# Seven block products for the third factor of a short convolution's input projection

## What is computed

```python
def short_conv_mixer(h, w_in, conv_w, w_out):
    bcx = h @ w_in                       # 512x1024 @ 1024x3072
    b_gate, c_gate, xp = bcx[..., :D], bcx[..., D:2*D], bcx[..., 2*D:]
    u = c_gate * xp
    u_conv = causal_depthwise_conv(u, conv_w)      # 3 taps along the tokens
    return (b_gate * u_conv) @ w_out

def swiglu(h, w_gate, w_up, w_down):
    return (silu(h @ w_gate) * (h @ w_up)) @ w_down

# layer 0: h = h + attention(rms_norm(h)); h = h + swiglu(rms_norm(h))
# layer 1: h = h + short_conv_mixer(rms_norm(h)); h = h + swiglu(rms_norm(h));  out = rms_norm(h)
```

## Time and profile before

| what | value |
|---|---|
| median of 3 runs | 1074.52 us (1074.01 to 1074.58) |
| the profiled execution, its own time | 1073.69 us |
| span of its instructions | 1071.9 us |
| PE busy | 1061.5 us, 99% of the span |
| PEld, DVE, ACT, POOL busy | 949.9, 777.4, 486.3, 40.5 us |
| chain of work that ended last | PE 91% |
| mean granted clock of TensorE | 0.996 of full speed |

### The profile page before, as it was taken

One profiled execution on the slowest core, in us unless ns is written; L12 is line 12 of the kernel. 1 busy time (PEld: TensorE's weight loads), 2 busy tenths in 40 slices (PEclk: granted clock), 3 DMA queues, 4 the chain that ended last, 5 costly groups with the idle time before them and its releaser, 6 DMA issues.

```text
span 1071.9 us, 17102 instructions
## 1 busy us (share of the span) xinstructions
PE 1061.5 (99%) x6496; PEld 949.9 (89%) x6496; DVE 777.4 (73%) x1081; ACT 486.3 (45%) x684; POOL 40.5 (4%) x22
## 2 busy tenths in 40 slices
PE   9999999999999999999999999999999999999997
PEld 7888888889999999888888888888999999988886
DVE  5667775999999998643457456779999999873343
ACT  6586663745554555422131212355545544651221
POOL 0232220000000000000000000000000000000000
PEclk9999999999999999999999999999999999999998
DMA  8221112232233322323322332322332233223301
GB/s 287 98 69 49 50 69 72 86 119 109 90 115 117 111 88 104 108 79 108 108 79 79 118 118 79 118 79 79 119 117 108 92 113 117 104 82 108 108 29 78
DMA packets 16959, 106.11 MB, mean 99 GB/s; under 512 B 1888, under 2 KB 2272, under 8 KB 6432
## 3 DMA queue, kind: packets, MB, share of 16 engines
q1 hardware_dynamic: 16848, 105.43, 27.4%
q0 software_dynamic: 80, 0.26, 0.2%
HBM read 103.59 MB, written 2.10 MB: 99 GB/s over the span
## 4 chain that ended last, share of the span: by engine, by line
PE 91%; DVE 2%; ACT 1%; issue 1%; DVEq 0%
PE bank L451 30%; PE bank L453 29%; PE bank L452 29%; PE bank L598 1%; PE bank L612 1%; ACT split L1034 1%; DVE s_lo L1513 0%; PE bank L782 0%; PE bank L490 0%; PE bank L600 0%; PE bank L496 0%; DVE work L1506 0%; DVE raw L1504 0%; DVE sq L1227 0%; DVE work L1501 0%
## 5 line engine op out<-in xcount | busy, mean ns | idle before, releaser
L795 ACT ACTIVATE split<-raw 128x2048 fp32r<-128x2048 f32 (+2 forms) x58 | 103.5, 1784 | 245.1 <-PE bank L453 241.2
L451 PE MATMUL bank<-x_hi,split 128*128 128x256 f32 (+1 forms) x704 | 204.2, 290 | 0.0
L452 PE MATMUL bank<-x_lo,split 128*128 128x256 f32 (+1 forms) x704 | 203.4, 289 | 0.0
L453 PE MATMUL bank<-x_hi,split 128*128 128x256 f32 (+1 forms) x704 | 203.4, 289 | 0.0
L1177 DVE TENSOR_TENSOR split<-raw,split 128x2048 fp32r<-128x2048 f32 (+2 forms) x50 | 108.6, 2171 | 103.3 <-ACT split L795 103.3
L453 PE MATMUL bank<-inner_hi,split 128*128 128x512 f32 x352 | 137.0, 389 | 0.0
L452 PE MATMUL bank<-inner_lo,split 128*128 128x512 f32 x352 | 137.0, 389 | 0.0
L451 PE MATMUL bank<-inner_hi,split 128*128 128x512 f32 x352 | 136.9, 389 | 0.0
L452 PEld LDWEIGHTS bank<-x_lo,split 128*128 128x128 f32 x704 | 132.3, 188 | 3.0 <-issue 0.5
L451 PEld LDWEIGHTS bank<-x_hi,split 128*128 128x128 f32 x704 | 132.3, 188 | 3.0 <-issue 0.5
L451 PE MATMUL bank<-x_hi,s_hi 128*128 128x256 f32 x480 | 134.3, 280 | 0.6 <-ACT work L1044 0.6
(11 more groups left out here) (201 smaller groups left out, 1913.6 us busy)
## 6 DMA issues: line engine op xcount, KB each, us to landing
raw<-weights_in SPq DMA_DIRECT2D x82, 1024.0 KB, 4.8
raw<-weights_in SPq DMA_DIRECT2D x12, 768.0 KB, 4.2
work<-x SPq DMA_DIRECT2D x4, 512.0 KB, 10.1
raw<-weights_in SPq DMA_DIRECT2D x4, 512.0 KB, 3.7
out<-head SPq DMA_DIRECT2D x3, 512.0 KB, 3.3
head<-head_in SPq DMA_DIRECT2D x1, 768.0 KB, 9.0
raw<-weights_in SPq DMA_DIRECT2D x3, 192.0 KB, 4.1
raw<-weights_in SPq DMA_DIRECT2D x1, 576.0 KB, 7.7
```

Of the source, the lines that this page charges most:

```text
L451: pe.matmul(o, lhs[0], rhs[0], start=start, stop=False, skip_group_check=True)
L452: pe.matmul(o, lhs[0], rhs[1], start=False, stop=False, skip_group_check=True)
L453: return pe.matmul(o, lhs[1], rhs[0], start=False, stop=stop, skip_group_check=True)
L795: act.activation(w_hi[s][:, 0:n], raw[s][:, 0:n], ACT.Copy).then_inc(hi_split[s], 1)
```

## The change

The x chunk of each of the four groups (third factor) goes through `winograd`, with its products in banks 4 to 7; B and C stay plain chunks. The order of chunks in the stream stays, and the x chunks' blocks are reordered on the host. Its token blocks are the operands `a_hi`, `a_lo` that are there already, plus the four differences (`conv_form`, then `tail_hi`, `tail_lo`), which ACT and DVE make during the last pair of the down projection of layer 0; for that DVE's two rounds are written out instead of looped. The rms is no longer applied to x: C is multiplied by `rstd2`, the square of `rstd`. The drains, the taps and the weight splits get a new order on ACT and DVE. `conv_mix` does what L1686 to L1694 did before, without the split of L1695. The diff, its core:

```diff
+TAIL_HI_AT, TAIL_LO_AT = ([FORMS_AT + n * TILE_BYTES for n in at] for at in ((10, 14, 2, 6), (12, 0, 4, 8)))
+MIX_AT = INNER_AT + 2 * KD * TILE_BYTES
...
+            def conv_block(k, form):
+                buf, c = (A, k * 2 * SEQ + form * HT) if form < X_T1 else (TAIL_FORMS[k], (form - X_T1) * HT)
+                return tuple(t[:, c:c + HT] for t in buf)
+
-            def winograd(s, b0):
+            def winograd(s, b0, x_of=x_block):
...
-            for c in range(12):
-                chunk(c % 2, [2 * (c % 3), 2 * (c % 3) + 1], A, ready=made if c == 0 else None)
+            for c in range(0, 12, 3):
+                chunk(c % 2, [0, 1], A, ready=None if c else made)
                 if c == 0:
                     stat(6, KD)
+                chunk((c + 1) % 2, [2, 3], A)
+                if c == 0:
+                    pe.wait_ge(x_split, T.add("x", K_PAIRS))
+                winograd(c % 2, GATE_BANK, conv_block)
...
+            def conv_scaled(k):
+                if k > 1:
+                    act.wait_ge(x_split, T.now("x") + k - 1)
+                for h in range(2):
+                    act.activation(tile(conv_form[k % 2], h), tile(xT, 2 * k + h), ACT.Copy, scale=gain("conv_norm", 2 * k + h)).then_inc(x_scaled, 1)
+            def conv_tail_hi(k):
+                act.wait_ge(x_formed, T.add("formed_x"))
+                act.activation(tail_hi[k][:, :], conv_form[k % 2][:, 2 * SEQ:X_PAIR], ACT.Copy).then_inc(x_hi_made, 1)
+            def conv_operands(c):
+                ks = {9: (0, 1), 10: (2,), 11: (3,)}.get(c, ())
+                for k in ks:
+                    conv_scaled(k)
+                for k in ks:
+                    conv_tail_hi(k)
...
             ffn(0)
-            for c in range(12):
-                if c % 3 == 2:
-                    for b in range(2):
-                        act.wait_ge(drained[4 + b], T.add(f"b{4 + b}"))
-                        act.activation(tile(work, 2 + b), tile(work, 4 + b), ACT.Copy,
-                                       scale=tap(CONV - 1, c // 3 * 2 + b)).then_inc(taps_started, 1)
-                split(c % 2)
-                if c == 0:
-                    rms(6, D)
+            idle_sqrt()
+            T.add("x", K_PAIRS)
+            act.wait_ge(stat_summed, T.add("stat"))
+            act.activation(rstd[:, :], bank[6][:, :], ACT.Sqrt, bias=eps[:, 0:1], scale=1.0 / D).then_inc(drained[6], 1)
+            def taps(m):
+                for b in range(2):
+                    act.wait_ge(u_made, m + b + 1)
+                    act.activation(mix_y[b], mix_u[b], ACT.Copy, scale=tap(CONV - 1, m + b)).then_inc(taps_started, 1)
+            for c in range(0, 12, 3):
+                s = c % 2
+                if c > 0:
+                    split(1 - s)
+                    taps(c // 3 * 2 - 2)
+                blocks_hi(s)
+                sums_hi_of(s)
+                split(1 - s)
+                copy(0, 1)
+                copy(0, 5)
+                copy(0, 6)
+                copy_last(0, s)
+            split(1)
+            taps(KD - 2)
...
+            def conv_forms(k):
+                b11, b12, b21, b22, t1, t2, t3, t4 = (conv_form[k % 2][:, n * HT:(n + 1) * HT] for n in range(X_FORMS))
+                v.wait_ge(x_scaled, T.add("scaled", 2))
+                do(v.tensor_tensor(t1, b12, b11, ALU.subtract))
+                do(v.tensor_tensor(t3, b22, b12, ALU.subtract))
+                settle()
+                do(v.tensor_tensor(t2, b22, t1, ALU.subtract))
+                settle()
+                v.tensor_tensor(t4, b21, t2, ALU.subtract).then_inc(x_formed, 1)
+            def conv_tail_rest(k):
+                v.wait_ge(x_hi_made, T.add("x"))
+                v.tensor_tensor(tail_lo[k][:, :], conv_form[k % 2][:, 2 * SEQ:X_PAIR], tail_hi[k][:, :], ALU.subtract).then_inc(x_split, 1)
...
+                def conv_operands(c):
+                    if c > 3:
+                        conv_tail_rest(c - 3)
+                    for k in {3: (0, 1), 4: (2,), 5: (3,)}.get(c, ()):
+                        conv_forms(k)
+                    if c == 3:
+                        conv_tail_rest(0)
...
                         if not (last and c >= 4):
                             split(c % 2, DOWN_AHEAD[c])
+                        if name and m:
+                            conv_operands(c)
...
+            def corners(s):
+                done(s)
+                b = GATE_BANK
+                v.wait_ge(drained[b], T.add(f"b{b}"))
+                drain(b + 3, v.tensor_tensor(u_half(1, 0), bank[b + 3][:, 0:HT], copies[0][0], ALU.add))
+                v.tensor_tensor(u_half(1, 1), copies[0][0], copies[0][1], ALU.add).then_inc(part_summed, 1)
+                v.wait_ge(part_summed, T.add("parts"))
+                for b in range(2):
+                    v.tensor_tensor(mix_u[b], mix_u[b], mix_y[b], ALU.mult).then_inc(u_made, 1)
+            def conv_mix(m):
+                v.wait_ge(u_made, m + 2)
...
+                inner_operands(m, mix_b)
+                all_ready()
...
+            forms(0)
+            conv_tail_rest(3)
+            forms_split(0)
+            v.wait_ge(drained[6], T.add("b6"))
+            do(v.reciprocal(rstd[:, :], rstd[:, :]))
+            settle()
+            done(0)
+            do(v.tensor_tensor(rstd2, rstd[:, :], rstd[:, :], ALU.mult))
+            settle()
+            drained_part(mix_b, 0, rstd[:, :])
+            for c in range(0, 12, 3):
+                s = c % 2
+                if c > 0:
+                    corners(1 - s)
+                    split(1 - s)
+                    conv_mix(c // 3 * 2 - 2)
+                    done(s)
+                    drained_part(mix_b, 0, rstd[:, :])
+                    forms(s)
+                    forms_split(s)
+                done(1 - s)
+                drained_part(mix_y, 2, rstd2)
+                split(1 - s)
+                top_left(0, u_half)
+                top_right(0, u_half)
+            corners(1)
+            split(1)
+            conv_mix(KD - 2)
+            clear_acc()
             mixer_out(CONV_OUT_BANKS)
```

More of the change, by code:

```diff
@@ L240, in build @@
         sums = work[:, 0:3 * BLOCK]
+        rstd2 = tile(work, 3)
+        mix_b, mix_y, mix_u = ([tile(mix, w + b) for b in range(2)] for w in (0, 2, 4))
         copies = [[t[:, g * HT:(g + 1) * HT] for t in (work[:, 5 * SEQ:6 * SEQ], acc, cos)] for g in range(2)]
@@ L708, in block_product @@
                     for k in range(K_PAIRS):
-                        c, n = block * BLOCK + k * P, k * X_PAIR + form * HT
-                        mm = product(bank[b][:, 0:HT], tuple(w[:, c:c + P] for w in weights),
-                                     tuple(x[:, n:n + HT] for x in X), start and k == 0, k == K_PAIRS - 1)
+                        c = block * BLOCK + k * P
+                        mm = product(bank[b][:, 0:HT], tuple(w[:, c:c + P] for w in weights), x_of(k, form),
+                                     start and k == 0, k == K_PAIRS - 1)
                     return mm
@@ L978, in _, with residuals @@
             banks_used(dict(b0=6, b1=2, b2=2, b3=3, b6=1, b7=4))
-            def residuals(banks, per, sizes, last=False, norm=None):
+            def conv_scaled(k):
[3 more added lines that the diff above has]
+                    act.activation(tile(conv_form[k % 2], h), tile(xT, 2 * k + h), ACT.Copy, scale=gain("conv_norm", 2 * k + h)).then_inc(x_scaled, 1)
+                T.add("scaled", 2)
+            def conv_tail_hi(k):
[7 more added lines that the diff above has]
+                    conv_tail_hi(k)
+            def residuals(banks, per, sizes, last=False, norm=None, also=None):
                 chunks = KD // 2 * per
@@ L1072, in gate @@
                 copy(0, 6)
-                copy_last(0)
+                copy_last(0, 0)
             def up():
@@ L1593, in winograd_round, with inner_operands @@
                 inner_product(f, 1, (UP_BANK + 3,))
-            def inner_operands(f, w):
+            def inner_operands(f, tiles):
                 for b in range(2):
-                    do(v.tensor_copy(at(u_hi, f + b), tile(work, w + b)))
+                    do(v.tensor_copy(tile(u_hi, f + b), tiles[b]))
                 settle()
                 for b in range(2):
-                    ready(lo(at(u_lo, f + b), tile(work, w + b), at(u_hi, f + b)))
+                    ready(lo(tile(u_lo, f + b), tiles[b], tile(u_hi, f + b)))
             def inner_rests(ms):
@@ L1650, in down_round @@
                             weigh(range(KD // 2, KD - 2))
[L1651 to L1656, removed]
+                down_round(0, False)
+                down_round(4, not name)
             clear_acc()
@@ L1660, in _, with u_half @@
             ffn("conv_norm")
[L1663 to L1681, removed]
+            def u_half(m, half):
+                return mix_u[m][:, half * HT:(half + 1) * HT]
@@ L1694, in _, with drained_part @@
                 settle()
-                inner_operands(m, 0)
```

(14 more changed lines are left out.)

34 lines of the change are left out of this document (23 added, 11 removed).

## The result

The changed kernel takes 1081.36 us, median of four runs (1080.21 to 1082.97), beside 1074.26 us for the kernel before on the same chip: a ratio of 1.0067, 95% interval 1.0054 to 1.0079. It is slower by 7 us where 1.8 us less were forecast. The profiled execution took 1081.16 us, 7.5 us more than that of before.

The account below looks back on a forecast made before the run. PE's own instructions were taken to bound the kernel, other engines counting only where PE waits. Saving 4.3 us and adding a 2.55 us wait gives -1.75 us, so 1074.52 becomes 1072.8 us, range 1071.5 to 1075.0.

Parts of the forecast that it names:

- the part on the forms: Under layer 0's down projection and the first group: ACT's and DVE's new work stays hidden, 3 us to spare.
- The rival that came in: Clock falls in PE's new 2.5 us gap before u tile 6, costing 1.4 to 2.7 us; chance 13%.
- The rival of DVE's chain missing the steady groups: PE waits three times for weights' rests or sums; 1077.3 us with 1.5 us lost per group; chance 4%.
- The step on the saving: On PE, each of four seven-product chunks takes 9.81 instead of 10.89 us: 1.08 us each, 4.3 us in all.
- The stage 127.4 us long: Sign of the forecast: the conv's input projection stage takes 127.4 us instead of 131.7.
- The steps on hidden work: First chunks and steady groups: operand tiles, weights and sums are ready before PE wants them, so no wait.
- The steady groups: Three groups, S being PE's first matmul after a seven-product chunk: weights and sums arrive hidden, 1.9 us to spare.
- The step on the added wait: Output projection: PE stands 2.55 us for u tile 6, as DVE's adds and weight split now precede it.
- The forecast of -1.75 us: Whole kernel: 4.3 us saved on PE less 2.55 us of added wait; chance of the forecast 72%.

Follow-up runs that it names:

- first: Changed kernel with DVE's wait done(0) moved ahead of forms_split(0) in front of the first group; 1072.81 us, ratio 0.9992 to the kernel before.
- last: Changed kernel with, in the last group alone, taps and u operands ahead of the weight split; 1078.14 us, ratio 1.0037 to the kernel before.
- swap: Changed kernel, done(0) ahead of forms_split(0), u operands before the last weight split, last group ordered B, x, C; 1068.07 us, ratio 0.9950.
- three: Changed kernel, done(0) ahead of forms_split(0), u operands before the last weight split, last x chunk plain again; 1070.37 us, ratio 0.9966.
- both: Changed kernel with done(0) ahead of forms_split(0) and, in the last group, operands before the weight split; 1070.78 us, ratio 0.9972.
- fill: Changed kernel, gaps kept, with 50 unread 128x256 matmuls in PE's first gap and 20 in the second; 1079.55 us, ratio 1.0048.

## Why the prediction was wrong

**The step that failed** is one place in the part on the forms: "With `rstd2` and two drains it ends near 572, the split for PE's next chunk near 574; PE wants it at 577.5. Hidden, 3 us to spare." It added up DVE's instructions between the reciprocal and that split and put a wait that stands among them, `done(0)` in the diff, at nothing without a word. That holds only if it waits for the plain chunk of slot 0, long done. What a counted wait of this program waits for is set by the last increment of its count, which is in the line above. With the wait in the right place the same instructions end at 574.6 (*first*), with 4.0 us to spare. (The sum was also off by two drains: four stand there, 577.38 to 580.14 in the timeline above, which is 1.4 us more than two; it was made up by a reciprocal that started earlier than forecast, 19.3 us behind the stage's start in *first* where 21 were taken.) The error is 6.1 us, and 2.7 more for the clock behind this gap; with 1.5 us for the clock behind the second gap that is the way from -1.75 us to the 8.5 us of the two stages.

**The rival that came in** is the clock. Its place, the second gap, and its price of "1.4 to 2.7 us" were right for the changed kernel's profile (1.55 us). It got 13%, as the prediction knew only the smaller gap and took dense work before and after a gap to speak against a fall. The traces don't bear that out: dense work stood on both sides of the 6.1 us gap, and the clock fell in both profiles that have it. The rival of DVE's chain missing the steady groups was not the one: PE has no wait there, in the changed kernel or in *first*.

**The step on the saving** (1.08 us a chunk) was right: 9.80 to 9.81 us per seven-product chunk, and 4.45 us off the stage where no gap spoils it, 1.11 a chunk. The Trainium skill's TensorE: Matmul & The Clock Gate, Back-to-back issue gap, whose sustained spacings spoke against the change, does not hold for this kernel's matmuls: by the prediction's estimate from it the four chunks would have lost 2 us or more. "The stage 127.4 us long" was 127.25 in *first*.

**The steps on hidden work** held: no wait of PE for operand tiles or weights near 553; the reciprocal from SBUF took 3.34 us, as from PSUM; ACT's 1024-column copy 1.06 against 1.1 taken. The steady groups were forecast with S + 1.55, S + 5.0 and weights and sums at S + 19.6 and S + 21.3. In the changed kernel S is 616.76 in the third group:

```profile
618.30 1.29 DVE L1766 TENSOR_TENSOR mix<-mix 128x512 f32<-128x512 f32 x2
...
621.72 1.41 DVE L1773 SCALAR_TENSOR_TENSOR mix<-mix,head 128x511 f32<-128x511 f32 x2
...
634.16 2.29 DVE L1591 TENSOR_TENSOR split<-raw,split 128x2048 fp32r<-128x2048 f32 x1 [1.98 <-ACT split L1081]
636.37 1.75 DVE L1597 TENSOR_TENSOR s_lo<-work,s_hi 128x1536 fp32r<-128x1536 f32 x1
```

These are S + 1.54 and S + 4.96 for the starts, S + 19.7 and S + 21.4 for the ends.

**The step on the added wait** was right to 0.03 us. It forecast 2.55 us before tile 6; PE's matmul due at 688.13 started at 690.66, 2.53 us late. DVE behind the last chunk, S = 679.95:

```profile
680.70 0.42 DVE L1762 TENSOR_TENSOR mix<-bank,work 128x256 f32<-128x256 f32 x1 [2.85 <-ACT work L1098]
...
682.70 2.29 DVE L1241 TENSOR_TENSOR split<-raw,split 128x2048 fp32r<-128x2048 f32 x1
684.90 1.41 DVE L1773 SCALAR_TENSOR_TENSOR mix<-mix,head 128x511 f32<-128x511 f32 x2
...
689.91 1.29 DVE L1284 TENSOR_TENSOR u_lo<-mix,u_hi 128x512 fp32r<-128x512 f32 x2
```

The split stands where the forecast put it, taps at S + 4.95, and the first tile's rest is there at 690.6. That it was the order and not the seven-product chunk itself is shown by *last* (0.5 us left of 2.4) and *swap* (nothing left).

The forecast of -1.75 us is thus what the kernel gives with its one misplaced wait put right and the clock full: -1.77 us in the profile of *first*. That it agrees to 0.02 us is luck: the stage saved 4.45 us where 4.3 were forecast, and the output projection lost 2.68 where 2.55 were.

## What to carry to other kernels

Where waits are counts kept by the program, work out for each wait in a changed order which increment it follows, before adding up the instructions around it. A margin of 3 us on paper is worth nothing if one line waits for the wrong chunk. When a chunk gets cheaper on the bounding engine but has a longer tail on the others, put it where a plain chunk follows: the last of the four seven-product chunks gave 1.1 us in the middle of its group (*swap* against *three*) and nothing right ahead of the output projection (*both* against *three*). A gap on TensorE can cost more than its length: 2.7 us on top of 6.1 here.

## What was not expected of the hardware

- The granted clock fell while PE stood for 6.1 us between dense stretches (in the changed kernel and in *last*). In the changed kernel it stayed at 0.50 for 5.5 us of dense work, 2.7 us lost for 6.1 us of gap; in *last* the mean was 0.54 over 5.3 us. With a gap of 2.5 us it fell in one profile (0.50 for 3.1 us, 1.55 us lost) and stayed full in another (*first*). With 0.5 to 0.7 us it stayed full (*last*, *both*). What decides at 2.5 us these runs don't tell. TensorE: Matmul & The Clock Gate, HAM oscillation, of the Trainium skill has gaps between groups of matmuls throttle the array; the trace agrees for 6.1 us, and *fill* shows that matmuls in the gap prevent it.
- DVE's two rounds of the down projection, written out instead of looped, run a little closer. From the scaled drain to the addition that waits for it:

```profile
542.90 0.68 DVE L1506 TENSOR_TENSOR work<-bank,rstd 128x512 f32<-128x512 f32 x1
543.62 0.69 DVE L1508 TENSOR_TENSOR head<-work,head 128x512 f32<-128x512 f32 x1
```

0.72 us, as in all eight such pairs of instructions, where the looped form of before had 0.84 to 0.87 in six of eight and 0.96 and 1.25 in the other two. It lies beside PE's work and changed nothing in the time; that the loop's waits are the cause was not tried.
